# Spreading a norm's reciprocal root over the partitions: a transpose of a repeated column in place of a product with the identity

## What is computed

```python
def rms_norm(x, g):
    xf = x.astype(jnp.float32)
    y = xf * lax.rsqrt(jnp.mean(xf * xf, axis=-1, keepdims=True) + EPS)
    return (y * g.astype(jnp.float32)).astype(x.dtype)
```

## Time and profile before

| | us |
|---|---|
| median of three runs | 853.43 |
| lowest, highest | 853.28, 855.17 |
| the profiled execution, its own time | 854.59 |
| span of the profiled execution | 852.8 |
| TensorE (PE) busy | 848.3 |
| weight loads (PEld) busy | 831.1 |
| DVE busy | 651.7 |
| ACT busy | 496.5 |
| POOL busy | 46.8 |

### The profile page before, as it was taken

One profiled execution on the slowest core, in us unless ns is written; L12 is line 12 of the kernel. 1 busy time (PEld: TensorE's weight loads), 2 busy tenths in 40 slices (PEclk: granted clock), 3 DMA queues, 4 the chain that ended last, 5 costly groups with the idle time before them and its releaser, 6 DMA issues.

```text
span 852.8 us, 17572 instructions
## 1 busy us (share of the span) xinstructions
PE 848.3 (99%) x7192; PEld 831.1 (97%) x7192; DVE 651.7 (76%) x1245; ACT 496.5 (58%) x905; POOL 46.8 (5%) x63
## 2 busy tenths in 40 slices
PE   9999999999999999999999999999999999999998
PEld 8999999999999898999999999999999999999998
DVE  6978668898977687576577555565899999997873
ACT  5786777764435667578778444343555564544650
POOL 0000000000000037000000000021020000000000
PEclk9999999999999999999999999999999999999999
DMA  9927878888977723287758855517546323566541
GB/s 302 347 63 239 265 226 257 265 270 280 307 258 238 256 99 100 83 253 225 217 167 216 257 183 186 191 41 201 170 150 198 99 76 100 163 210 193 157 145 50
DMA packets 162864, 164.22 MB, mean 193 GB/s; under 512 B 16816, under 2 KB 159328, under 8 KB 162528
## 3 DMA queue, kind: packets, MB, share of 16 engines
q1 hardware_dynamic: 161696, 162.05, 60.3%
q10 hardware_dynamic: 1088, 1.05, 0.4%
HBM read 162.01 MB, written 2.91 MB: 193 GB/s over the span
## 4 chain that ended last, share of the span: by engine, by line
PE 97%; DVE 1%; DMA 1%; ACT 0%; POOL 0%; ACTq 0%; issue 0%; DVEq 0%
PE ps L316 25%; PE ps L318 25%; PE ps L320 25%; PE ps L442 3%; PE ps L1595 2%; PE ps L1597 2%; PE ps L1593 2%; PE ps L1654 2%; PE ps L459 2%; PE ps L1689 1%; PE ps L1691 1%; PE ps L1693 1%; PE ps L1635 1%; PE ps L1644 1%; PE ps L1133 1%; PE ps L1142 1%
## 5 line engine op out<-in xcount | busy, mean ns | idle before, releaser
L283 DVE TENSOR_TENSOR wl<-raw,wh 128x1024 fp32r<-128x1024 f32 x256 | 309.2, 1224 | 26.9 <-ACT wh L276 26.7
L316 PE MATMUL ps<-xh,wh 128*128 128x256 f32 x1136 | 319.6, 281 | 0.0
L320 PE MATMUL ps<-xh,wl 128*128 128x256 f32 x1136 | 315.0, 277 | 0.0
L318 PE MATMUL ps<-xl,wh 128*128 128x256 f32 x1136 | 314.9, 277 | 0.0
L276 ACT ACTIVATE wh<-raw 128x1024 fp32r<-128x1024 f32 x256 | 267.1, 1051 | 73.2 <-PE ps L320 66.5
L316 PEld LDWEIGHTS ps<-xh,wh 128*128 128x128 f32 x1136 | 213.8, 188 | 2.1 <-issue 1.0
L318 PEld LDWEIGHTS ps<-xl,wh 128*128 128x128 f32 x1136 | 213.7, 188 | 0.4 <-DVE xl L384 0.2
L320 PEld LDWEIGHTS ps<-xh,wl 128*128 128x128 f32 x1136 | 213.5, 188 | 0.0
L320 PE MATMUL ps<-hh,wl 128*128 128x256 f32 x512 | 141.3, 276 | 0.0
L316 PE MATMUL ps<-hh,wh 128*128 128x256 f32 x512 | 141.3, 276 | 0.0
L318 PE MATMUL ps<-hl,wh 128*128 128x256 f32 x512 | 141.3, 276 | 0.0
(11 more groups left out here) (358 smaller groups left out, 1414.3 us busy)
## 6 DMA issues: line engine op xcount, KB each, us to landing
raw<-in_w_in_dram SPq DMA_DIRECT2D x34, 1024.0 KB, 5.2
raw<-in_mlp_up_dram SPq DMA_DIRECT2D x32, 1024.0 KB, 5.5
raw<-in_mlp_down_dram SPq DMA_DIRECT2D x32, 1024.0 KB, 7.1
aw<-in_w_adaT_dram SPq DMA_DIRECT2D x24, 512.0 KB, 5.1
raw<-in_rec_w_in_dram SPq DMA_DIRECT2D x7, 1024.0 KB, 11.6
raw<-in_att_w_in_dram SPq DMA_DIRECT2D x6, 1024.0 KB, 5.6
raw<-in_rec_w_out_dram SPq DMA_DIRECT2D x4, 1024.0 KB, 6.1
raw<-in_att_w_o_dram SPq DMA_DIRECT2D x4, 1024.0 KB, 5.0
```

The source lines that it names most:

```text
L283: e.tensor_tensor(parts_of(i)[1], raw_of(i), f32(parts_of(i)[0]), op=ALU.subtract).then_inc(S["wl"], 1)
L316: e.matmul(o, H[:, first + n], xh[:, k], start=start and n == 0, stop=False)
L318: e.matmul(o, H[:, first + n], xl[:, k], start=False, stop=False)
L320: ins = e.matmul(o, L[:, first + n], xh[:, k], start=False, stop=stop and n == len(ks) - 1)
```

## The change

In all eight places the product with the identity is replaced by a matmul in transpose mode, with the same operands: the repeated column is turned. Its transpose has the column's values along the free dimension, on every partition, which is the same tile. `start` and `stop` are dropped. Nothing else changes.

```diff
     def rms_spread_pe(e, q, r):
         p = claim(q, AUX[1], (S["rs"], r + 1))
         q.wait_ge(S["rst"], r + 1)
-        e.matmul(p[:, 0:128], RST[:, 0:1].to_broadcast([128, 128]), ident, start=True, stop=True)
-        e.matmul(p[:, 128:256], RST[:, 1:2].to_broadcast([128, 128]), ident, start=True, stop=True).then_inc(
+        e.matmul(p[:, 0:128], RST[:, 0:1].to_broadcast([128, 128]), ident, is_transpose=True)
+        e.matmul(p[:, 128:256], RST[:, 1:2].to_broadcast([128, 128]), ident, is_transpose=True).then_inc(
             closing(f"spread{r}", p), 1)
...
         for blk in range(2):
             ins = e.matmul(p[:, blk * 128:blk * 128 + 128], CRS[:, blk:blk + 1].to_broadcast([128, 128]), ident,
-                           start=True, stop=True)
+                           is_transpose=True)
         ins.then_inc(closing("cspread", p), 1)
...
         for b in range(4):
             ins = e.matmul(p[:, b * 128:(b + 1) * 128], FR[:, b:b + 1].to_broadcast([128, 128]), ident,
-                           start=True, stop=True)
+                           is_transpose=True)
         ins.then_inc(closing("fspread", p), 1)
...
             for blk in range(2):
                 ins = e.matmul(p[:, blk * 128:blk * 128 + 128], LR[:, blk:blk + 1].to_broadcast([128, 128]), ident,
-                               start=True, stop=True)
+                               is_transpose=True)
             ins.then_inc(closing("lns", p[:, 0:256]), 1)
```

## The result

The changed kernel took 860.57 us (median of 6 executions, 860.18 to 865.21) against 853.36 (6, 852.37 to 855.17) of the kernel before on the same chip: ratio 1.0094, interval 1.0069 to 1.0120. The prediction was 852.1 with a range of 850.9 to 854.9. So it was wrong, and on the side to which it had given one chance in ten. The profiled execution took 860.18 us, its span is 858.4 (854.59 and 852.8 before).

A forecast was written before the change was run, and what follows sets the result against it. The prediction took TensorE, busy for 99% of the span, as the bound; six places at 0.22 us sum to 1.32 us, bringing the median from 853.43 to 852.1 us, range 850.9 to 854.9.

The forecast's parts named there:

- what a record is worth: Step pricing each record saved at a spread: 0.68 against 0.46 us, so 0.22 for two instructions, 0.11 each.
- rows 4: Profile rows of TensorE around L1662's pair of transposes, 727.08 to 727.54: 0.46 us, taken as the pattern for the new spreads.
- A loss is excluded: Bound on a record's worth at the spreads: never below nothing, since the pattern with transposes is the shorter one.
- Rival 1: Products behind the MLP spreads run at the slow pace, 4.3 ns more a record, 6.4 us behind the first; 864.7; chance 0.09.
- The rival's sum of three spreads: Slow pace behind all three MLP spreads, 6.4 + 1.3 + 4.9 us: 12.6 us, giving 864.7.
- the 0.45 us around the spread: At the first-layer MLP spread, the second product behind was forecast to start 0.46 us after the one before it.
- the first norm's saving swallowed at L459: First norm, 16.5 us: its 0.22 us counted as 0, idle time ahead of L459 growing up to 0.5.
- the final norms' at L1595: Final norms, 556.2 us: their 0.45 us counted as 0, the wait ahead of L1595 growing from 0.3 to 0.7.
- The sum of 1.32 us: Saving counted at six places, MLP, attention, latent, context and layer norm spreads, 0.22 us each; bounds 0 and 2.0.
- Rival 2: Slow stretch of 695 records around the final norms becomes fast: 3.0 us less, 849.1; chance 0.03.
- Rivals 3 and 4: 3: all eighteen instructions count, 2.0 us, 851.4, chance 0.04. 4: transposes still make two records, 853.4, chance 0.03.
- Rival 5: The 24 products behind each of five spreads run at half clock: 13.6 us added, 865.7; chance 0.01.

The follow-up runs named there:

- bench2: TensorE alone, whole computation left out: 48-record streams between groups of short matmuls, each group entered in three states; 1172.54 us, one run.
- two_late_ln: two_late with the layer norm's spread put back to plain fp32 products; 853.62 us, ratio 0.9990 to the kernel before.
- r1_only: The kernel before with only the spread of the first-layer MLP norm turned into transposes; 860.08 us, ratio 1.0068.
- one_late: The changed kernel with the transposed spreads r = 1, 3 and 4 issued one record later; 859.86 us, ratio 1.0046.
- mixed_moves: The changed kernel with r = 1 sum and spread one record later, r = 3 sum one later, r = 4 spread two later; 859.48 us, one run.
- mlp_plain: The changed kernel with the spreads r = 1, 3 and 4 put back to plain products with the identity; 854.36 us, ratio 1.0009.
- last_plain: The changed kernel with only the second matmul of the spreads r = 1, 3 and 4 put back to a plain product; 855.69 us, ratio 1.0014.
- two_late: The changed kernel with the transposed spreads r = 1, 3 and 4 issued two records later; 853.91 us, ratio 1.0002 to the kernel before.
- bench: TensorE alone, whole computation left out: streams of 48 records with groups of short matmuls between them, no waits; 564.52 us, one run.
- two_late_more: two_late_ln with two added transposed pairs that compute nothing; 852.33 us, ratio 0.9981 to the kernel before.

## Why the prediction was wrong, point by point

**The step that failed** is in what a record is worth: "What precedes and follows is the same in both, so no switch of mode is left out: it is inside the 0.46. ... I take 0.11 because rows 4 are the very pattern." They weren't. L1662 turns a dense tile, the new spreads turn a column repeated 128 times, and bench2 has the two apart: from the mark second to last, which is what the spread at 104 meets, the dense tile leaves fast and the repeated column slow. The kernels show it too. Groups of TensorE's weight loads in the kernel before, 724.2 to 727.1 us, ahead of the very pair of rows 4:

```profile
L318 PEld LDWEIGHTS ps<-xl,wh 128*128 128x128 f32 x8 | 1.5, 192 | 0.0
L316 PEld LDWEIGHTS ps<-xh,wh 128*128 128x128 f32 x8 | 1.5, 188 | 0.0
L320 PEld LDWEIGHTS ps<-xh,wl 128*128 128x128 f32 x8 | 1.5, 188 | 0.0
```

The mark is on L318, second to last, just as ahead of the spread at 104, and this pair leaves fast. In the twelve profiled kernels that compute, the dense pairs that stand alone in the stream (L1662 at 727 us and the last of L1162 at 353 us in the kernel before) met the mark there 24 times and left fast 24 times. "A loss is excluded" fails with it: the pattern with transposes was the shorter one, and the loss lay behind it. The 0.22 us themselves were right (0.23 measured). What the prediction missed is the switch, 4.5 ns on each of 1484 records.

**Rival 1** was the case that came, with its price of 6.4 us against 6.7 measured and its own sign ("if the first long stretch, from 105 to 273, comes out slow"). With 6.4 and 1.3 us on the forecast it gives 859.8, against 860.57 measured. But its condition, that transposes do not set the fast pace, was right in part only, and that it held behind the first two spreads was luck: the same two instructions left fast behind the context spread, and dense ones do everywhere. Nor does the pace switch at short matmuls alone, as it says: the stall at 356.6 us, in the same trace, switched it too. It had 0.09 because of the fast stretch from 728 to 768, again behind the dense tile. Against that stood a row that I had seen and read too lightly: the stream's pace changed exactly where the edited instructions stand, and nothing in the profile said what about them made it change. With two long stretches hanging on an unexplained switch, and one analogue for its outcome, the chance should have been nearer to one in three and the range should have reached 861. The rival's sum of three spreads was too much in the typical execution: the context spread met the mark last, since the second-layer stretch had turned slow ahead of it, and left fast. In the two executions at 864.8 and 865.2 it may have been the other way round: the 142 steps slow (+0.6), which leaves the mark last ahead of the second-layer spread; its stretch fast (-1.4), the context's slow (+5.2). On the 860.4 of the other four that makes 864.8; they were not profiled.

**Right:** 18 records; the 0.45 us around the spread; the first norm's saving swallowed at L459 (0.3 to 0.5 us) and the final norms' at L1595 (longest wait 0.3 to 0.4, a second one beside it, 0.6 in all). One reading there was off: the final spread starts at 556.17, a little before the chain leaves TensorE at 556.37 and not after it; it stands behind the product from which the chain leaves, so nothing hung on this. The sum of 1.32 us can be checked now: the six savings measure 1.4 in the changed kernel. And the profiled execution of two_late_ln has every long stretch at its pace of before, and one saving less (the layer norm's 0.22). Forecast for it is 1.10; its span is 851.5 against 852.8, 1.3, of which 0.1 was gained ahead of the first spread.

**Rival 2** meant the stretch from 553.5 to 635.1, and did not come (692 records there in the changed kernel, 695 before); that a slow stretch can become fast was seen at 362, in a small way. **Rivals 3 and 4** did not come. **Rival 5**, the clock: the granted clock is 1.00 in every stretch shown, behind transposes too; so no row here shows the drop that the prediction drew from the Trainium skill (page "TensorE: Matmul & The Clock Gate", section Part 4: PE-mode transpose). The Trainium skill (same page, section Terms) calls the transpose mode four times as fast for fp32; the trace does not agree, it shows a factor of two: one record for two, 0.11 us for 0.22.

**Open:** the layer norm's turned spread meets the mark last in all six profiles that have it with this operation, and leaves fast in three (the changed kernel, one_late, mixed_moves) and slow in three (mlp_plain, last_plain, two_late). There TensorE stands 0.3 us between the last product and the spread, so something finer than the mark must count. For the spreads r = 1, 3 and 4 no such exception was seen: 25 turned pairs in nine profiled kernels, 11 with the mark second to last, all slow; 14 with it last or first, all fast. The other exception is the sum of r = 2, ahead of which TensorE stalls 0.3 to 0.4 us in three steps: it left fast in the changed kernel and in r1_only, and slow in the other ten, with the mark in either of two places. What the mark is inside the engine no run shows.

## What to carry to other kernels

Where a stream of back-to-back weight loads and products fills TensorE, compare its records per microsecond in each stretch between groups of short matmuls, at equal clock: two paces 4% apart may be in it, and an edit worth 0.2 us at such a group can decide the pace of the next 170 us. Price such an edit by the stretch behind it. Before giving up an operation that is cheaper but leaves slow, try it one and two records further on, in an accumulation of another bank, and choose the place that is fast from both states in which it can be entered.

## What the runs showed of the hardware that was not expected

- A stream of 128x256 products with a new 128x128 weight load each runs at 113.3 or 117.8 ns a record at granted clock 1.00, and holds either for as long as neither a group of short matmuls nor a stall interrupts it (1484 records). In the slow pace one load in three shows 192 ns and the others 188.
- The pace has a memory across groups. In bench and bench2 a sum pair entered fast leaves the mark second to last ahead of a group 48 records on (42 of 42), one entered slow leaves it last (82 of 82).
- Two transposes of a repeated column leave slow from one place of the mark in three; two of a dense tile from none; a single one of a repeated column from the last place and from a fast stream, three from the last place.
- Work that computes nothing can pay: in two_late_more two added transposes at 77 us turned 154 slow steps fast, 0.4 us less with their own cost counted. The 1.3 us between the medians of two_late_more and two_late_ln are not all theirs.
